# Hybrid decoder layer in float32 pairs: one of three weight sums of the up-projection moved from an adding transfer to VectorE

## The reference, cut to what matters

```python
def conv_glu_ffn(h, w_up, conv_w, conv_b, w_down):
    u = h @ w_up                                   # (512, 2048) @ (2048, 11264)
    c = lax.conv_general_dilated(u, conv_w[:, None, :], window_strides=(1,),
                                 padding=[(CONV_WIDTH - 1, 0)], ...) + conv_b   # causal, depthwise, width 3
    gate, val = jnp.split(c, 2, axis=-1)
    return (jax.nn.gelu(gate, approximate=True) * val) @ w_down
```

## Time and profile before

| | |
|---|---|
| median of three runs | 2002.81 us |
| the profiled execution | 2000.05 us, of which its span 1998.1 us |
| merged chunks, 3 to 20 | about 810 to 1522 us of the span |
| TensorE busy (matmul) | 1966.3 us, 98% |
| VectorE busy | 1475.0 us, 74% |
| ScalarE busy | 1012.6 us, 51% |
| GpSimd's adding transfers | 57 of 1 MB, 14.9% of the DMA engines' time |

### The profile page before, as it was taken

How to read it: one execution, slowest core, us unless ns; L and a number is a source line. 1 busy time by engine, 2 the same in 40 slices (tenths; PEclk the granted TensorE clock), 3 DMA queues, 4 the chain that set the end, 5 groups by cost and what they waited for, 6 DMA issues and landing times.

```text
span 1998.1 us, 27810 instructions
## 1 busy us (share of the span) xinstructions
PE 1966.3 (98%) x10408; PEld 1678.4 (84%) x10408; DVE 1475.0 (74%) x2044; ACT 1012.6 (51%) x1539; POOL 55.1 (3%) x65
## 2 busy tenths in 40 slices
PE   8999999999999999999999999999999999999998
PEld 6888888888887889888888888888889887888786
DVE  4343544445436899788888888888888998889888
ACT  6442323435435764555555555555555655555454
POOL 0000000000000000000000000000000000000000
PEclk9999999999999999999999999999999999999999
DMA  9462322221646534777877787887786997877675
GB/s 383 147 223 94 102 90 64 85 64 64 241 133 200 185 121 162 195 194 209 230 198 198 216 228 192 205 227 210 200 207 193 310 323 233 276 244 242 214 265 202
DMA packets 229108, 388.02 MB, mean 194 GB/s; under 512 B 11842, under 2 KB 139970, under 8 KB 219120
## 3 DMA queue, kind: packets, MB, share of 16 engines
q1 hardware_dynamic: 219520, 320.19, 47.8%
q0 software_dynamic: 8208, 59.77, 14.9%
q10 hardware_dynamic: 1248, 6.29, 0.8%
HBM read 286.30 MB, written 44.07 MB: 165 GB/s over the span
## 4 chain that ended last, share of the span: by engine, by line
PE 85%; DVE 9%; issue 2%; ACT 2%; DMA 0%; DVEq 0%; ACTq 0%
PE ring L2514 15%; PE ring L2270 13%; PE ring L2272 12%; PE ring L2271 12%; PE ring L2516 8%; PE side L2514 7%; PE side L2516 3%; DVE w_lo L1906 3%; PE side L2270 3%; PE side L2271 2%; PE side L2272 2%; PE side L2346 1%; PE side L2319 1%; DVE f L2116 1%; PE side L2329 1%
## 5 line engine op out<-in xcount | busy, mean ns | idle before, releaser
L1605 DVE TENSOR_TENSOR w_lo<-raw,w_hi 128x512 fp32r<-128x512 f32 x256 | 169.5, 688 | 270.5 <-ACT w_hi L1122 270.3
L2514 PE MATMUL ring<-s,w_hi 128*128 128x512 f32 x864 | 306.2, 397 | 2.3 <-ACT snaps L1441 2.2
L1906 DVE TENSOR_TENSOR w_lo<-raw,w_hi 128x1024 fp32r<-128x1024 f32 x216 | 253.3, 1173 | 74.4 <-ACT w_hi L1332 55.9
L1906 DVE TENSOR_TENSOR w_lo<-q,w_hi 128x1024 fp32r<-128x1024 f32 x218 | 255.4, 1172 | 44.0 <-ACT w_hi L1332 27.1
L1122 ACT ACTIVATE w_hi<-raw 128x512 fp32r<-128x512 f32 x256 | 151.1, 622 | 198.2 <-PE ring L2272 193.8
L2516 PE MATMUL ring<-s,w_lo 128*128 128x256 f32 x864 | 242.0, 280 | 0.0
L1332 ACT ACTIVATE w_hi<-q 128x1024 fp32r<-128x1024 f32 x176 | 185.1, 1055 | 51.6 <-PE side L2516 46.0
L2514 PE MATMUL ring<-a,w_hi 128*128 128x512 f32 x576 | 202.6, 396 | 0.0
L2270 PE MATMUL ring<-w_hi,act_hi 128*128 128x512 f32 x488 | 193.0, 395 | 9.2 <-DVE w_lo L1605 8.7
L2514 PEld LDWEIGHTS ring<-s,w_hi 128*128 128x128 f32 x864 | 162.0, 188 | 44.3 <-ACT snaps L1441 6.2
L1332 ACT ACTIVATE w_hi<-raw 128x1024 fp32r<-128x1024 f32 x130 | 135.1, 1056 | 112.4 <-DVE raw L1609 78.4
(11 more groups left out here) (331 smaller groups left out, 4360.0 us busy)
## 6 DMA issues: line engine op xcount, KB each, us to landing
q<-in_w_up SPq DMA_DIRECT2D x65, 1024.0 KB, 5.4
raw<-in_w_in SPq DMA_DIRECT2D x24, 1024.0 KB, 5.2
raw<-in_w_up SPq DMA_DIRECT2D x23, 1024.0 KB, 8.3
q<-q POOLq DMA_DIRECT2D x19, 1024.0 KB, 6.9
q<-raw POOLq DMA_DIRECT2D x19, 1024.0 KB, 6.9
raw<-q POOLq DMA_DIRECT2D x19, 1024.0 KB, 7.3
q<-in_w_down SPq DMA_DIRECT2D x66, 256.0 KB, 4.7
raw<-in_w_down SPq DMA_DIRECT2D x66, 256.0 KB, 4.4
```

The source lines that it names most:

```text
L1605: dve.tensor_tensor(w_lo[:, s, q], raw[:, s, q], w_hi[:, s, q].bitcast(F32), ALU.subtract).then_inc(lo_done, 1)
L1906: dve.tensor_tensor(lo, src, hi.bitcast(F32), ALU.subtract).then_inc(hp_lo_done, 1)
L2514: pe.matmul(bank.rearrange("p (h n) -> p h n", h=2), b_hi, hi_lo, start=first, stop=False, skip_group_check=True)
```

## The change

VectorE makes T4 in the merged chunks (and chunk 21) as it does in chunks 0 to 2: `make_t(c, "T4")` in `after` of step 5, behind lo(9) and ahead of `c11_paired`. GpSimd's third adding transfer goes. Who waited for the semaphore `t4_in` now waits for `t_done`, which counts two sums for each of these chunks in place of one.

```diff
         def t_count(c, name):
 
             if c < PAIRED[0]:
                 order = ("T1", "T3", "T2", "T4") if c == 0 else ("T1", "T2", "T3", "T4")
                 return 4 * c + order.index(name) + 1
-            return 4 * PAIRED[0] + c - PAIRED[0] + 1
+            return 4 * PAIRED[0] + 2 * (c - PAIRED[0]) + ("T2", "T4").index(name) + 1
 
         def t_ready(c, name):
 
-            if c >= PAIRED[0] and name != "T2":
-                return {"T1": t1_in, "T3": t3_in, "T4": t4_in}[name], 16 * (c - PAIRED[0] + 1)
+            if c >= PAIRED[0] and name in ("T1", "T3"):
+                return {"T1": t1_in, "T3": t3_in}[name], 16 * (c - PAIRED[0] + 1)
             return t_done, t_count(c, name)
...
                                raw[:, 0, :], accum_op=ALU.add).then_inc(t3_in, 16)
-                pool.wait_ge(hp_lo_done, place(c, P6, 1) + 1)
-                pool.wait_ge(*b_landed("21", c))
-                pool.dma_start(raw[:, 1, :], b21_at(c)[:, :, :].rearrange("p k n -> p (k n)"),
-                               accum_op=ALU.add).then_inc(t4_in, 16)
...
                 if c < CHUNKS:
-                    if s == 5 and c < PAIRED[0]:
+                    if s == 5:
                         make_t(c, "T4")
```

More of the change, by code:

```diff
@@ L584, in build @@
         t_done, t1_in, t3_in = sem("t_done"), sem("t1_in"), sem("t3_in")
-        t4_in, c12_done, c11_folded = sem("t4_in"), sem("c12_done"), sem("c11_folded")
+        c12_done, c11_folded = sem("c12_done"), sem("c11_folded")
         c21_folded, c22_folded = sem("c21_folded"), sem("c22_folded")
```

## The result

The changed kernel takes 2034.61 us (median of 4 runs, 2034.18 to 2035.91) against 2003.8 us before in the same runs: ratio 1.0157, 95% interval 1.0145 to 1.0169. It is slower by some 31 us. Its profiled execution took 2035.91 us, of which the span is 2034.1.

What follows compares the result with a forecast made beforehand. The T2-to-T2 loop through VectorE, ScalarE and T1's transfer was taken to bound, not TensorE. Eighteen periods of 41.52 us give 747.4 against 711.8, 35.6 late, less 1.0 at the end: 2002.81 + 34.6 = 2037.4 us, range 2024 to 2046.

Steps and rivals of the forecast that it cites:

- The loop: Merged chunks, T2 to next T2 through VectorE, ScalarE and T1's transfer: 39.11 us, said to bind in place of TensorE.
- D: Rival at T1's transfer: it gets quicker once T4's transfer is gone; 2003 us, chance 0.02.
- B: Rival at step 10: ScalarE, not the fold, is late, so T4 fills 0.68 us there; 2025 us, chance 0.08.
- A: Rival in VectorE's waits: idle time takes T4; 2003 us, or 1995 with 0.43 us a chunk regained; chance 0.10.
- The price of T4 in a chunk: VectorE between lo(9) and `c11_paired`: T4 delays everything to lo(1) and the next T2 by 2.21 us.
- The way over T1: From lo(1)'s end through T1's transfer to the next T2: forecast 7.55 us, between 7.35 and 7.99 seen before.
- rival C: The stretch from lo(1) to T2 is slow, 7.99 us, in all chunks: 8 us more, 2045 us, chance 0.06.
- my signs of being wrong: Period near 39.5, T1 landing under 6 us, a fold ScalarE isn't waiting for, or TensorE waiting elsewhere, lo(10) first.
- TensorE's stall: TensorE at step 6, from chunk 4 on: waits about 2.3 us each for ScalarE's copy, 41.5 less 39.2.
- Chunk 21 and what follows: T4 of chunk 21 costed at nothing, at most 2.2 us; TensorE's spare 1.0 us comes off; down-projection's length unchanged.
- I carry the difference: From profiled execution to median: the 2.76 us between them before was added again, 2034.7 becoming 2037.4 us.
- The two rules weighed: Skill's rules, both rejected: occupancy makes 19 sums free, 2003 us; transfer fit gives T1 4.4 us, not the measured 6.99.

## Why the prediction was right

*The loop.* Right, and shown. Half of T1's transfer, another order, and a sum of the same length in the transfer's place moved the time as the loop says, between 2034 and 2000, while VectorE's work stayed the same or grew; half the sum gave half the loss. T4's absence did not speed T1 up (D: the median from issue to landing is 6.9 us in both kernels), and hi(10) did wait for the fold (B: ScalarE idle 6.13 us there). The idle time did not take the sum (A), but for the part in the next paragraph.

*The price of T4 in a chunk.* 2.21 us forecast; the way from T2 to lo(1) went from 31.76 to 33.93, which is 2.17. But 31.76 was not the length in every chunk. In ten of the eighteen it was 32.08 to 32.23, because lo(1) waited 0.26 to 0.41 us for its hi half, which stands in ScalarE's order behind a copy that waits for TensorE. The chunk of the earlier trace rows is one:

```profile
918.72 0.38 ACT L1444 ACTIVATE u_val<-ring 128x256 f32<-128x256 f32 x1 [1.48 <-PE ring L2516]
919.00 1.05 ACT L1332 ACTIVATE w_hi<-q 128x1024 fp32r<-128x1024 f32 x1
```

The prediction's "No wait for TensorE stands anywhere in it" holds for the chunk that it followed, and not for these. After the change none of the eighteen has this wait: T4 filled it, and the mean cost on this way is 33.93 - 31.97 = 1.96 us. The forecast is not hurt by it, since it added T4 to the shortest chunk and compared with the measured mean.

*The way over T1.* 7.55 forecast as the mean, and measured 41.56 - 33.93 = 7.63. That it came so near is partly luck, for it is made differently: 7.3 in 14 of 18 chunks, 7.68 in one, and 8.96, 8.97 and 9.40 in three. The kernel before had six at 7.8 to 8.05 and none that long; rival C, 7.99 in all chunks, did not come. Where it was longest, T2 came so late that lo(4) held TensorE at step 4 as well:

```profile
1018.29 2.29 DVE L1605 TENSOR_TENSOR raw<-raw,q 128x2048 f32<-128x2048 f32 x1 [4.35 <-DMA q<-q]
```

```profile
1023.14 0.47 PE L2510 MATMUL ring<-s,w_hi 128*128 128x512 f32 x1 [1.72 <-DVE w_lo L1902]
```

A wait of TensorE on another line was among my signs of being wrong, lo(10) first; it was lo(4), three times, 4.3 us in all, and it comes behind the loop and not in place of it. T4's transfers don't make the ways slow (their removal left it). What does isn't settled, but the trace has a lead: in each of the three slow ones a 16 KB transfer on queue 8, which the profile calls "instruction", starts 6.4 to 6.9 us behind T1's issue, and T1 lands 8.5 to 9.0 us behind it. In the fourteen at 7.3, T1 lands at 6.9, and no such transfer starts between the issue and the landing, except one right at the landing. Whether it is the cause no run tested.

*TensorE's stall.* 2.3 us a chunk was forecast, from an own time of 39.2 for a merged chunk (39.54 - 8.4 / 18 is 39.07, so 39.2 was a loose rounding). Against a chunk without waits, 39.57, a quiet chunk of the changed kernel takes 1.65 us more. The time lost in its stalls is larger, since part of its steps ran at the quicker rate of the last section: where the starts of two pairs of matmuls lie more than 0.38 us apart, they exceed the usual 0.35 by 37.8 us over the eighteen chunks, 2.1 each. The wait rows did not come out as I said: "from some 8 to about 40 us" took 8.4 as the sum of 2.2 at the matmul and 6.2 at the weight load, and the same sum is now 22.5 + 34.8 = 57.3. The two count largely the same idle time. VectorE's wait for T1 is 2.23 us in a quiet chunk, 2.1 forecast, and 2.54 in the mean with the slow ways. The total came out all the same, since it was taken from periods, not from stalls.

*Chunk 21 and what follows.* Costed at nothing, and 476.1 us both times, but as a sum of small things. The 1.0 us of TensorE's spare time did show at step 6:

```profile
1569.73 0.39 PE L2516 MATMUL ring<-s,w_hi 128*128 128x256 f32 x1 [0.71 <-ACT snaps L1458]
```

That is 34.97 us later than in the earlier trace rows, where T2 of the chunk is 35.98 later. It did not last. About 0.3 us went at the start of the down-projection, where TensorE's weight load waited 0.5 us for VectorE and 0.2 before (VectorE's 1.61 us of the earlier trace rows are gone there, so T4 of chunk 21 cost that much), and 0.4 near 2005 us, where VectorE had waited longer for loads of weights; that these loads came later because of the change isn't shown. In the end the spans differ by 36.0 us and the eighteen loops by 36.2, and the 0.26 us between the two starts of T2 in chunk 3 make up the rest.

*The sum.* For the profiled execution 2034.7 was forecast and 2035.91 measured. For the median it was 2037.4 against 2034.61. The difference between the two forecasts was my step "I carry the difference" of 2.76 us from the one profiled execution before to the median, and that did not hold: the changed kernel's profiled execution is above its median. The kernel before spreads over 2001.19 to 2005.55 in 27 runs, and the profiled one, 2000.05, was quicker than all of them. In medians taken together the change cost 30.8 us where I had 34.6. What spreads the runs was not looked into.

*The two rules weighed.* The Trainium skill's occupancy rule (Perfetto Trace Analysis, Identifying the Most-Contended Engine), as I applied it, pointed at 2003, and the runs disagree: VectorE at 86% came with a loss of 31 us, at 95% with none. I had quoted TensorE's 98%, which is matmul time; the section judges TensorE's headroom by the busy share of the weight loads instead. In the merged chunks that is 616.89 of 712 us, 87%, still ahead of VectorE's 85, so it points the same way. T1's adding transfer landed 6.9 us after its issue at 1 MB and 4.5 at half (medians of 19 each), which makes 2.1 us fixed and 4.8 us for each MB, as an estimate from the two sizes. The Trainium skill's fit (DMA: Bandwidth & Descriptors, Anatomy of one DMA) has 2.0 us fixed, which agrees, and 2.4 for each MB, half of what this adding transfer shows.

## What to carry to other kernels

When one engine is at 98% and another has 15% free, follow one recurring instruction (here T2) to its next occurrence through every engine and transfer and add up: if that loop is as long as the bounding engine's period, each microsecond put into it is lost once per turn, whatever the busy shares say. Sort the helper's idle intervals into those that wait for the bounding engine, which give way by themselves, and those that wait for its own earlier results, which don't but can be filled by an independent operation put just there. And a transfer that nobody waits for is worth nothing when removed; the one to replace here was T1's, which is in the loop, for about 3 us (0.13%, interval 0.9978 to 0.9996 against the kernel before).

## What the runs showed of the hardware that I had not expected

TensorE's pair of matmuls, 512 and 256 columns, came at two rates at the same granted clock of 1.00. In the four runs where TensorE waits for nothing in the merged chunks, one takes 39.57 us, 112 pairs at 0.353 us, and the quicker rate does not appear there. The kernel before did some chunks in 39.11 us with T2 to T2 set by the loop, and TensorE there came through a step of 8 pairs in 2.77 us in place of 2.83: the first matmuls of its steps 6 and 10, at 1258.63 and 1269.83, are 11.20 us apart, four times 2.77 and 0.1 lost at the first pair, where four steps take 11.31 in the steady runs. In that trace the longest quicker stretch began at about 1180 us and ended at about 1376, at a stall of 0.49 us. The changed kernel has steps of both kinds. What sets the rate isn't settled; no run here varied it.
